# Convolution taps split over three engines, and the router's small sums given to TensorE, in a fused two-block transformer kernel

## The reference

```python
def second_block(...):
    mod = cond @ mod_w[l] + mod_b[l]
    sh1, sc1, g1, sh2, sc2, g2 = ...
    h = _rmsnorm(x, norm1_g[l]) * (1 + sc1) + sh1
    z = h @ w_in[l]
    a_val, a_gate, cq, ckv, qi, ki, wi, u_pool = jnp.split(z, split_at, axis=-1)
    y_conv = _conv_module(a_val, a_gate, ...)      # 31-tap depthwise conv of 256 channels, layernorm, silu
    y_att = _dsa_attention(cq, ckv, qi, ki, wi, ...)  # 8 index heads choose 64 keys; 8 heads attend to them
    y_pool = _pool_mixer(u_pool, ...)
    mix = jnp.concatenate([y_conv, y_att, y_pool], axis=-1) @ w_out[l]
    x = x + g1 * mix
    h = _rmsnorm(x, norm2_g[l]) * (1 + sc2) + sh2
    x = x + g2 * _hier_moe(h, ...)                 # router: 4 groups + 32 experts; 3 x 64 MB of expert weights
```

## Time and profile before

| | |
|---|---|
| median of 3 runs | 944.02 us (942.58 to 944.15) |
| the profiled execution's own time | 944.15 us |
| its span in the profile | 942.4 us |
| PE busy | 789.0 us (84%) |
| DVE, ACT, POOL busy | 348.7, 313.3, 125.5 us |
| transfers | 297.95 MB, mean 316 GB/s |

### The profile page before, as it was taken

One profiled execution on the slowest core, in us unless ns is written; L12 is line 12 of the kernel. 1 busy time (PEld: TensorE's weight loads), 2 busy tenths in 40 slices (PEclk: granted clock), 3 DMA queues, 4 the chain that ended last, 5 costly groups with the idle time before them and its releaser, 6 DMA issues.

```text
span 942.4 us, 12391 instructions
## 1 busy us (share of the span) xinstructions
PE 789.0 (84%) x5204; PEld 523.6 (56%) x5204; DVE 348.7 (37%) x767; ACT 313.3 (33%) x623; POOL 125.5 (13%) x129
## 2 busy tenths in 40 slices
PE   9999999999999999999899997557665576756765
PEld 7985578999998867778786443113220222211213
DVE  6746765777765554398523011010100101001002
ACT  5665655766665476313632100001000000000012
POOL 0011031444441042101311000000000000000000
PEclk9999999999999999999999998989888988788868
DMA  9955971755534476544559999999999999999995
GB/s 352 408 213 216 431 301 54 276 188 190 187 124 179 179 268 248 222 179 160 198 206 411 403 428 426 428 428 428 427 428 428 428 427 428 427 429 426 430 426 208
DMA packets 24110, 297.95 MB, mean 316 GB/s; under 512 B 2672, under 2 KB 3056, under 8 KB 5488
## 3 DMA queue, kind: packets, MB, share of 16 engines
q1 hardware_dynamic: 24048, 297.09, 77.3%
HBM read 296.03 MB, written 1.05 MB: 315 GB/s over the span
## 4 chain that ended last, share of the span: by engine, by line
PE 58%; DMA 32%; DVE 4%; ACT 4%; issue 1%; POOL 0%; DVEq 0%; ACTq 0%; POOLq 0%
PE ps L107 58%; DMA ring<-in_exps 32%; ACT fr L116 1%; DVE ar L125 1%; ACT ar L116 1%; PE ps L110 1%; ACT ar L113 1%; DVE misc L148 1%; ACT sq L113 1%; DVE fr L125 0%; DVE yT L125 0%; DVE yT L129 0%; DVE sq L130 0%; DVE rb L136 0%; DVE hT L133 0%
## 5 line engine op out<-in xcount | busy, mean ns | idle before, releaser
L107 PE MATMUL ps<-ring,sq 128*32 128x512 f32 x944 | 137.7, 719 | 74.1 <-DMA ring<-in_exps 73.7
L107 PE MATMUL ps<-fr 128*128 128x256 f32 (+1 forms) x956 | 164.8, 325 | 1.1 <-DVE fr L125 1.1
L107 PEld LDWEIGHTS ps<-fr 128*128 128x128 f32 x956 | 141.6, 192 | 16.9 <-ACT fr L116 1.2
L107 PE MATMUL ps<-ring,ar 128*32 128x512 f32 (+3 forms) x792 | 104.0, 614 | 45.1 <-DMA ring<-in_exps 39.3
L107 PEld LDWEIGHTS ps<-ring,sq 128*32 128x32 f32 x944 | 28.7, 121 | 171.1 <-DMA ring<-in_exps 117.7
L125 DVE TENSOR_TENSOR ar<-ar,ps 128x512 f32<-128x512 f32 x9 | 6.2, 688 | 255.1 <-PE ps L107 255.1
L125 DVE TENSOR_TENSOR fr<-ring,fr 128x512 fp32r<-128x512 f32 (+1 forms) x96 | 77.7, 828 | 50.6 <-ACT fr L116 50.3
L116 ACT ACTIVATE ar<-ps 128x512 f32<-128x512 f32 (+4 forms) x48 | 27.2, 571 | 176.1 <-PE ps L110 142.5
L107 PEld LDWEIGHTS ps<-ring,ar 128*32 128x32 f32 (+1 forms) x792 | 27.2, 119 | 104.5 <-DMA ring<-in_exps 58.4
L116 ACT ACTIVATE fr<-ring 128x512 fp32r<-128x512 f32 (+1 forms) x114 | 66.6, 624 | 26.3 <-PE ps L107 23.6
L107 PE MATMUL ps<-ar 128*128 128x512 f32 (+9 forms) x320 | 64.1, 420 | 10.9 <-DVE ar L125 10.1
(11 more groups left out here) (188 smaller groups left out, 928.2 us busy)
## 6 DMA issues: line engine op xcount, KB each, us to landing
ring<-in_exps SPq DMA_DIRECT2D x86, 2048.0 KB, 30.9
ring<-in_modw SPq DMA_DIRECT2D x12, 2048.0 KB, 8.9
ring<-in_wup SPq DMA_DIRECT2D x11, 2048.0 KB, 9.1
ring<-in_wdown SPq DMA_DIRECT2D x5, 2048.0 KB, 7.6
ar<-in_exps SPq DMA_DIRECT2D x5, 2048.0 KB, 12.8
ring<-in_win SPq DMA_DIRECT2D x4, 2048.0 KB, 7.6
ring<-in_exps SPq DMA_DIRECT2D x6, 1024.0 KB, 8.1
ring<-in_wo SPq DMA_DIRECT2D x2, 2048.0 KB, 9.9
```

Source lines behind the costliest of these rows:

```text
L107: return Issue(self.e and self.e.matmul(o, l, r, start=start, stop=stop, skip_group_check=True))
```

## The change

1. The conv's taps of channel block 1 leave DVE. ACT makes tap 0 with the bias into `acc[1]`, and scales the input by each further tap's weight into one of six scratch tiles (`wT2`); POOL adds these to `acc[1]`. ACT's 31 instructions stand between the copies and relus that it has in this stage. Block 0 stays on DVE, now as one chain in which each instruction waits for the one before. PE's `mu` waits for both.
2. The router's bias is made by PE alone: eight matmuls with the column of `sh`, broadcast, as weights. POOL's product and DVE's reduction are gone. The matmuls stand before `mix_parts(0, (0, 1))`.
3. On PE, `mix_parts(0, (6, 7))` moves ahead of `dsa_scores(3)`, `turn` 2 ahead of `mix_parts(1, (6, 7))`; the products of tiles 0 to 3 with blocks 2 and 3 and those of tile 4 with six blocks leave the attention's stretch and follow it. ACT copies `at` 0 two steps later.
4. The squares are added up by PE: one matmul a tile with 32 columns of ones, in four quadrants of the partitions; ACT copies the result out of PSUM into `sums`. POOL's six sums and DVE's one are gone.

The core of the diff:

```diff
@@ tensor @@
-            pe.wait_ge(dve_conv["tap", 30, 1], act_in2["relu", 2])
+            pe.wait_ge(pool_conv["tap", 30], dve_conv["tap", 30], act_in2["relu", 2])
...
+            pe.wait_ge(dve_mod["mod", 2], act_conv["vd", 0])
+            for k in range(8):
+                t = pe.matmul(ps[:, 7, 0:36], sh[:, k:k + 1].broadcast_to([128, 128]), rw3[:, k, :], k == 0, k == 7)
+            t.then_inc(pe_out2, "rbias")
             pe.wait_ge(loaded("wout2", 0), act_conv["mix", 1], act_conv["qa", 2])
             mix_parts(0, (0, 1))
             turn("dsa", 0, dsa_s[0])
             pe.wait_ge(act_out2["pool", 1])
             mix_parts(1, (0, 1))
-            pe.wait_ge(dve_out2["rsum"], act_conv["vd", 0])
-            pe.matmul(ps[:, 7, 0:36], ones, rsum, True, True).then_inc(pe_out2, "rbias")
             dsa_scores(2)
             turn("dsa", 1, dsa_s[1])
+            mix_parts(0, (6, 7))
+            dsa_scores(3)
             values("dsa", 0, dsa_p[0], vd, act_conv["vd", 1], act_conv["qa", 3])
-            dsa_scores(3)
-            mix_parts(0, (6, 7))
             values("dsa", 1, dsa_p[1], vd)
+            turn("dsa", 2, dsa_s[0])
             mix_parts(1, (6, 7))
-            turn("dsa", 2, dsa_s[0])
-            pe.wait_ge(act_out2["at", 0])
-            mix_parts(0, (2, 3))
             values("dsa", 2, dsa_p[0], vd, dve_out2["rbias"])
             turn("dsa", 3, dsa_s[1])
-            mix_parts(1, (2, 3))
             values("dsa", 3, dsa_p[1], vd)
-            pe.wait_ge(loaded("wout2", 1))
-            for kk in (0, 1, 6, 7, 2, 3):
-                mix_product(bank(6, 0, S), 6, 2, kk, 0, False)
...
+            def tile_squares(k):
+                q = 32 * (k % 4)
+                pe.wait_ge(act_out2["xsq", k])
+                pe.matmul(ps[q:q + 32, ST, 0:S], ones[:, 0:32], tile(sq, k % 4), k < 4, k >= 4).then_inc(pe_out2, "squares", k)
...
-            for k in range(4):
-                wout2_tile(k, (4, 5))
+            for i in range(2):
+                for n in range(2):
+                    wout2_tile(2 * i + n, (2, 3, 4, 5))
...
-            pe.wait_ge(dve_out2["squares"])
+            pe.wait_ge(act_route["sums"])
@@ scalar @@
+            def taps(lo, hi):
+                for k in range(lo, hi):
+                    o = ar[:, wT2 + S * (k % 6):wT2 + S * (k % 6) + S]
+                    act.wait_ge(dve_in2["glu"], pool_conv["tap", k - 6] if k > 6 else None)
+                    act.copy(o, upad[:, 1, k:k + S], col("conv_k2", 31 + k)).then_inc(act_conv, "tap", k)
...
+            act.activation(acc[1], upad[:, 1, 0:S], ACT.Identity, scale=col("conv_k2", 31), bias=col("conv_b2", 1)).then_inc(act_conv, "tap", 0)
+            taps(1, 11)
             for j in range(2):
                 act.wait_ge(pe_in2["qi", j])
                 act.copy(ar[:, qi + 512 * j:qi + 512 * j + 512], bank(2 + j)).then_inc(act_in2, "qi", j)
+                taps(11 + 8 * j, 19 + 6 * j)
...
                 act.activation(as2(ar[:, rel + 768 * (i % 2):rel + 768 * (i % 2) + 768]), two(2 * (i % 2)), ACT.Relu).then_inc(act_in2, "relu", i)
+                taps(25 + i, 26 + i)
+            taps(29, 31)
...
             shares("dsa", 2, dsa_s[0], 0.125)
-            dsa_out(0)
             shares("dsa", 3, dsa_s[1], 0.125)
             turned("dsa", 2, dsa_p[0])
+            dsa_out(0)
...
+            act.wait_ge(pe_out2["squares", 7], act_out2["at", 1], pool_conv["pm"], pool_conv["rwg"])
+            act.copy(sums, half(ST, 0)).then_inc(act_route, "sums")
@@ vector @@
-            for k in range(1, 31):
-                for c in range(2):
-                    dve.wait_ge(dve_conv["tap", k - 1, c])
-                    dve.scalar_tensor_tensor(acc[c], upad[:, c, k:k + S], col("conv_k2", 31 * c + k), acc[c], ALU.mult, ALU.add).then_inc(
-                        dve_conv, "tap", k, c)
+            for k in range(1, 31):
+                dve.wait_ge(t)
+                t = dve.scalar_tensor_tensor(acc[0], upad[:, 0, k:k + S], col("conv_k2", k), acc[0], ALU.mult, ALU.add).then_inc(dve_conv, "tap", k)
@@ gpsimd @@
+            for k in range(1, 31):
+                pool.wait_ge(t, act_conv["tap", k], act_conv["tap", 0])
+                t = pool.tensor_tensor(acc[1], acc[1], ar[:, wT2 + S * (k % 6):wT2 + S * (k % 6) + S], ALU.add).then_inc(pool_conv, "tap", k)
```

More of the change, by code:

```diff
@@ L964, in tensor @@
                 tile_logits(p)
+                tile_squares(p)
             for k in range(4, 8):
-                wout2_tile(k, (4, 5) if k == 4 else (0, 1, 6, 7, 2, 3, 4, 5))
+                if k == 4:
+                    pe.wait_ge(loaded("wout2", 1))
+                wout2_tile(k, (0, 1, 6, 7, 2, 3, 4, 5))
                 for p in {4: (2,), 5: (3,), 6: (4, 5)}.get(k, ()):
                     tile_logits(p)
+                    tile_squares(p)
             tile_logits(6)
+            tile_squares(6)
+            tile_squares(7)
+            tile_logits(7)
             def token_major(n):
@@ L1439, in scalar @@
             act.activation(sig, bank(1), ACT.Sigmoid).then_inc(act_in2, "gate")
+            act.wait_ge(dve_in2["glu"])
+            act.activation(acc[1], upad[:, 1, 0:S], ACT.Identity, scale=col("conv_k2", 31), bias=col("conv_b2", 1)).then_inc(act_conv, "tap", 0)
+            taps(1, 11)
             for j in range(2):
@@ L1509, in scalar @@
             for k in range(8):
-                act.wait_ge(dve_out2["x", k], pool_out2["squares", k - 4] if k > 4 else None)
-                act.activation(tile(sq, k % 4) if k else sums, tile(xT, k), ACT.Square).then_inc(act_out2, "xsq", k)
+                act.wait_ge(dve_out2["x", k], pe_out2["squares", k - 4] if k > 3 else None)
+                act.activation(tile(sq, k % 4), tile(xT, k), ACT.Square).then_inc(act_out2, "xsq", k)
+            act.wait_ge(pe_out2["squares", 7], act_out2["at", 1], pool_conv["pm"], pool_conv["rwg"])
+            act.copy(sums, half(ST, 0)).then_inc(act_route, "sums")
             act.wait_ge(pe_route["cols"])
-            row_root(misc[:, 112:114], ps[:, ST, S:S + 2], 1024).then_inc(act_route, "root")
+            row_root(misc[:, 112:114], ps[:, ST, S:S + 2], 32 * 1024).then_inc(act_route, "root")
             act.wait_ge(dve_route["rh"], pe_out2["logits", 7])
@@ L1900, in vector @@
             dve.wait_ge(t)
-            for c in range(2):
-                dve.tensor_scalar(acc[c], upad[:, c, 0:S], col("conv_k2", 31 * c), col("conv_b2", c), ALU.mult, ALU.add).then_inc(
-                    dve_conv, "tap", 0, c)
+            t = dve.tensor_scalar(acc[0], upad[:, 0, 0:S], col("conv_k2", 0), col("conv_b2", 0), ALU.mult, ALU.add).then_inc(dve_conv, "tap", 0)
             for k in range(1, 31):
-                for c in range(2):
-                    dve.wait_ge(dve_conv["tap", k - 1, c])
-                    dve.scalar_tensor_tensor(acc[c], upad[:, c, k:k + S], col("conv_k2", 31 * c + k), acc[c], ALU.mult, ALU.add).then_inc(
-                        dve_conv, "tap", k, c)
+                dve.wait_ge(t)
+                t = dve.scalar_tensor_tensor(acc[0], upad[:, 0, k:k + S], col("conv_k2", k), acc[0], ALU.mult, ALU.add).then_inc(dve_conv, "tap", k)
             t = [None, None]
@@ L1961, in vector @@
                 maxima("dsa", i, dsa_s[i], dsa_mask, 0.125)
-            dve.wait_ge(pool_conv["rwsh"])
-            dve.reduce(rsum, rwsh.rearrange("p (k n) -> p n k", n=36), ALU.add).then_inc(dve_out2, "rsum")
             for i in range(2):
@@ L1977, in vector @@
                 dve.scalar_tensor_tensor(tile(xT, k), bank(b, o, o + S), mod[:, 16 + k:17 + k], tile(xT, k), ALU.mult, ALU.add).then_inc(dve_out2, "x", k)
-            dve.wait_ge(pool_out2["squares", 6], act_out2["xsq", 7])
-            dve.tensor_tensor(sums, sums, tile(sq, 3), ALU.add).then_inc(dve_out2, "squares")
             dve.wait_ge(act_route["root"])
@@ L2205, in gpsimd @@
                                    gc.rearrange("p (k o) -> p k o", o=1).broadcast_to([128, 8, 36]), ALU.mult).then_inc(pool_conv, "rwg")
-            for k in range(1, 7):
-                pool.wait_ge(t, act_out2["xsq", k], act_out2["xsq", 0])
-                t = pool.tensor_tensor(sums, sums, tile(sq, k % 4), ALU.add).then_inc(pool_out2, "squares", k)
             for g in range(GROUPS):
```

9 lines of the change are left out of this document (2 added, 7 removed).

## The result

The changed kernel ran in 955.18 us (median of four, 953.57 to 956.45), beside 944.09 for the kernel before in the same comparison (942.58 to 946.53): 1.0096 of it, interval 1.0067 to 1.0124. It is slower. Its profiled execution took 951.65 us, with a span of 949.8. The profiled one is 3.5 us under the median, and that is no accident: 32 executions of this kernel are recorded, 17 of them from 950.54 to 952.18 us and 15 from 953.57 to 957.02. All four that make the median belong to the upper group, the profiled one to the lower; the median of all 32 is 952.05. The last experiments are about the difference between the groups.

A forecast was written before the change was run, and what follows sets the result against it. PE's arrival at the first expert products was taken to bound the kernel, the weight stream having no reserve. Terms -0.7, +3.5, +2.6, +0.75 and +1.7 gave +7.9 us on 944.02: 951.9 us, range 949.2 to 956.4.

The forecast's parts named there:

- The bound: Weight stream without reserve at slot 12: each microsecond PE comes later to its first expert products (509.54) delays the end equally.
- the six slots: Expert-weight loads between the stream's restart at 481.58 and slot 12: 29.4 us, lasting to 511.0.
- Part 1, +1.7: Conv taps moved to ACT and POOL: PE 1.7 us later, 0.45 without disturbance, up to 6.2 at 1.05 a pair.
- The pair every 0.88 us: Conv stage: DVE taps and POOL sums disturb each other and take turns, one of each every 0.88 us.
- The rule as the prediction quotes it: Conv stage: DVE with two SBUF inputs contends with GpSimd reading SBUF; the second is blocked throughout; 1.2 us of the sum.
- DVE's lateness: After the conv: DVE 2.7 us late at its reciprocals; less 0.5 and 0.6 of slack, PE 1.6 to 1.7 late.
- PE's own path: After the conv: PE 1.15 us late, 0.7 waiting for the copies ki and wit and 0.45 for relu 1.
- Parts 2 and 3, +2.8 (-0.7 and +3.5): Router bias and attention order: tiles start 0.7 us earlier, then 48 mixing products instead of 40 cost 3.5.
- The three waits: PE in the attention: 2.0 us before the third transpose, 1.0 before the last values, about 0.7 before the block.
- Part 4, +2.6 and +0.75: Squares on PE: six matmuls before tile 7's end at 0.43 us each, 2.6; 0.75 more behind tile 7.
- The clock: Rival: new PE gaps bring 1.2 GHz for 4 us, PE loses 2 us, giving 953.9 us; chance 0.11.
- The other rivals: No DVE and POOL disturbance, 950.7 us (0.12); 1.05 us a pair, 956.4 (0.15); stream alone decides, 943.0 (0.07).

The follow-up runs named there:

- The last experiments: Changed kernel with small unread matmuls in PE's gaps: 949.99 us; changed kernel repeated: 951.29; kernel before with PE-made router bias and such matmuls: 941.23.
- the late restart: Kernel before, with the loads of experts 7, 8, 9 and 6 waiting in addition for output tile 1: 948.77 us, ratio 1.0039.
- three in which it is 1 to 2 us more: Kernel before with PE squares in two rows of four: 1.0007; with taps offloaded, POOL's sums left out: 945.00 us; taps offloaded, DVE's sum in PSUM: 944.38.
- Part 1 alone: Kernel before with only the conv taps of channel block 1 moved to ACT and POOL: 947.38 us, ratio 1.0032.
- part 3 alone: Kernel before with only the attention reordered and eight mixing products moved behind it: 947.28 us, ratio 1.0043.
- three other kernels: Kernel before with conv taps offloaded: 947.38 us; the same with DVE's running sum in PSUM: 944.38; kernel before with only the attention reordered: 947.28.

## Why the prediction was right

Slower, and 951.9 us is the time of the lower group of runs (950.54 to 952.18); the median of 955.18 lies inside the range. That it came so close is in part luck: mis-sized parts cancel, and which half-clock stretches an execution has, 1.7 us each, was no part of the sum. Step by step:

- **The bound.** Right. The end followed PE's first expert products, net 430.6 to 431.4 us behind them in ten of the fourteen kernels' profiles, before and after among them; the other four are the one with the late restart and three in which it is 1 to 2 us more, with no cause found. But the two rows of PE's products at 509.54 (1.92) and slot 12 at 511.50 were misread: 0.86 of the 1.92 us was half clock. Without it slot 12 is due at 510.64, against 511.0 for the six slots. By that count the stream would be last by 0.4 us, by the late restart it had 0.8 of reserve: at full clock the two are within 1 us, and which is last is not settled.
- **Part 1, +1.7.** The pair every 0.88 us was right (0.87), `ki`'s delay too (0.7, measured 0.68). The rule as the prediction quotes it, that the later instruction is blocked for the whole of the other, is not borne out in full: 0.48 and 0.73 us in turns would be 1.21 a pair. The sum was +0.97. The term that failed is DVE's lateness. Part 1 alone, DVE at the reciprocals:

```profile
440.98 0.22 DVE L136 RECIPROCAL misc<-misc 128x2 f32<-128x2 f32 x2
```

  It was ready for them 2.1 us later (measured from the conv's first step), not 2.7, since only 0.55 of it arose in the taps, and 0.9 of it was slack, the 0.49 and a second gap of 0.28 with its reciprocal. PE's own path (1.0, forecast 1.15) decided, and the 0.6 of slack at the latent covered the rest.
- **Parts 2 and 3, +2.8 (-0.7 and +3.5).** The -0.7 for the start of the tiles holds part 2's 0.7 already, so the sum gave part 3 no earlier start of its own. Measured: -0.79 for part 2 and +3.17 for part 3, together +2.38. In part 3 alone the tiles start 0.3 earlier, and tile 7 ends 3.45 later behind their start. The three waits were forecast at 2.0, 1.0 and about 0.7: they measured 1.92, 0.90, 0.71.
- **Part 4, +2.6 and +0.75:** +4.0 and +0.86. This is the mis-sized term. The prediction took a full product's 0.43 us as the upper bound of a lone narrow one; it costs 0.67. Neither row that bounded it, a full product and narrow ones beside their like, was of a narrow one alone.
- The errors cancel: -0.7 in part 1, -0.4 in parts 2 and 3, +1.5 in part 4. Net +8.29 for a forecast of +7.9, and slot 12 at 519.73 for 519.4.
- **The clock.** The rival (0.11: one stretch of 4 us, 2 us lost) was right in size, 3.4 us and 1.7, and wrong in being one case: the profiled execution has one, others several, and the kernel before has them too. Its chance was read from the one stretch at the earlier trace rows that had a clock of 1.00, without asking where in the same trace it was 0.50; in three other kernels the clock fell behind that very gap. The clock is the likely reason why the median is 3.3 us above the forecast: the one profile from the upper group has the stretches, but none of the four executions of the median was profiled.
- The other rivals fell: DVE and POOL do disturb each other, a pair takes 0.87 and not 1.05, and the stream did not decide alone, since the end moved with PE.

## What to carry to other kernels

Work moved from a DVE that is not late to POOL can cost time on both, if both read two SBUF tensors; putting the running sum in PSUM takes the contention away. Where PE is the bound, giving it small sums costs PE's time, and a narrow matmul alone between full-width ones costs more than a full one: put narrow ones in a row of different quadrants, or outside the stretch. Before pricing anything from a PE row, look at the granted clock of its stretch. And when a kernel's times fall into two groups, a median of four can come from one of them alone.

## What the runs showed of the hardware

- PE's clock fell to 1.2 GHz for about 3.4 us (once for 6.8) behind gaps of PE of 0.3 to 2.3 us in some executions and not in others of the same kernel: before at 148 and 509, after at 474 or at 147 to 153, 423, 478 and 522. Each costs up to 1.7 us. The two profiles of that kernel, with one stretch and with four, differ by 5.7 us. With the gap of 1.92 us filled by eight matmuls the stretch was absent in the one execution profiled.
- A lone matmul of 32 output columns by 256 between full-width ones: 0.67 us; of 128 columns: 0.43; four of 32 in different quadrants in a row: 0.17 each.
- DVE multiply-adds and POOL sums of 256 fp32 columns, side by side in SBUF: 0.83 and 0.79 us each in place of 0.48 and 0.73, a pair every 0.87.
